# Low-rank attention of a two-block network: value products of two key tiles in the two column halves of the array, softmax denominators from GpSimd's sums

## The reference

```python
def mla_block(qn, qr, kn, kr, v):
    s = (jnp.einsum('bqhd,bkhd->bhqk', qn, kn) + jnp.einsum('bqhr,bkr->bhqk', qr, kr)).astype(jnp.float32) * MLA_SCALE
    p = jax.nn.softmax(s, axis=-1).astype(v.dtype)
    return jnp.einsum('bhqk,bkhd->bqhd', p, v)

def mla_latent(qn, qr, kn, kr, v):
    out = lax.map(lambda a: mla_block(a[0], a[1], kn, kr, v), (to_blocks(qn), to_blocks(qr)))
    return from_blocks(out)
```

## Time and profile before

| | us |
|---|---|
| median of the runs shown (3 runs) | 4291.66 |
| lowest, highest | 4281.98, 4299.93 |
| the profiled execution | 4297.97 |
| its span in the trace | 4296.1 |
| stage of the change, layer 0 (506.9 to 775.0) | 268.1 |
| stage of the change, layer 1 (1913.5 to 2154.3) | 240.8 |

### The profile page before, as it was taken

One profiled execution on the slowest core, in us unless ns is written; L12 is line 12 of the kernel. 1 busy time (PEld: TensorE's weight loads), 2 busy tenths in 40 slices (PEclk: granted clock), 3 DMA queues, 4 the chain that ended last, 5 costly groups with the idle time before them and its releaser, 6 DMA issues. The chain is left out here.

```text
span 4296.1 us, 51403 instructions
## 1 busy us (share of the span) xinstructions
PE 3948.0 (92%) x20691; PEld 3101.0 (72%) x20691; DVE 2079.7 (48%) x3243; ACT 1274.4 (30%) x2169; POOL 511.4 (12%) x601
## 2 busy tenths in 40 slices
PE   7989899988999899989996998899778999999997
PEld 5889565666777679866665998687555688887875
DVE  3466566333222256556535332683664465553444
ACT  3225433231111042553313333312453211112241
POOL 1010211102222110021012111100102100000011
PEclk9999899999999999889997999899788999999998
DMA  6100000448877431000025996112001211112111
GB/s 254 35 20 1 17 1 1 176 173 342 284 276 276 147 140 38 1 17 1 1 89 231 340 342 225 71 49 89 3 1 69 74 49 46 48 50 81 49 57 59
DMA packets 73876, 453.29 MB, mean 106 GB/s; under 512 B 8000, under 2 KB 12624, under 8 KB 57680
## 3 DMA queue, kind: packets, MB, share of 16 engines
q1 hardware_dynamic: 56960, 389.73, 24.1%
q0 software_dynamic: 13088, 47.19, 4.0%
q10 hardware_dynamic: 3632, 13.63, 0.8%
HBM read 394.95 MB, written 55.57 MB: 105 GB/s over the span
## 5 line engine op out<-in xcount | busy, mean ns | idle before, releaser
L2349 PEld LDWEIGHTS psum<-words,words 128*128 128x128 f32 x4096 | 510.9, 191 | 10.3 <-issue 9.1
L2349 PE MATMUL psum<-words,words 128*128 128x160 f32 (+1 forms) x4096 | 512.2, 287 | 1.6 <-DVE words L398 0.9
L682 PE MATMUL psum<-words,words 128*128 128x512 f32 x1104 | 440.7, 399 | 14.2 <-DVE words L722 9.8
L684 PE MATMUL psum<-words,words 128*128 128x512 f32 x1104 | 437.4, 396 | 0.0
L683 PE MATMUL psum<-words,words 128*128 128x512 f32 x1104 | 436.9, 396 | 0.0
L682 PEld LDWEIGHTS psum<-words,words 128*128 128x128 f32 x1104 | 208.7, 189 | 66.9 <-DVE words L722 11.4
L1658 PE MATMUL psum<-words,words 128*128 128x428 f32 (+1 forms) x720 | 253.2, 352 | 4.0 <-DVE words L1751 4.0
L1366 PE MATMUL psum<-words 128*128 128x512 f32 (+1 forms) x504 | 254.0, 586 | 0.0
L1659 PE MATMUL psum<-words,words 128*128 128x428 f32 (+1 forms) x720 | 248.7, 345 | 0.0
L1660 PE MATMUL psum<-words,words 128*128 128x428 f32 (+1 forms) x720 | 248.2, 345 | 0.0
L701 ACT ACTIVATE words<-words 128x1024 fp32r<-128x1024 f32 x69 | 73.1, 1060 | 581.0 <-DMA words<-in_w_up 382.2
(11 more groups left out here) (441 smaller groups left out, 7844.5 us busy)
## 6 DMA issues: line engine op xcount, KB each, us to landing
words<-in_w_gate SPq DMA_DIRECT2D x32, 2048.0 KB, 8.1
words<-in_w_up SPq DMA_DIRECT2D x32, 2048.0 KB, 12.5
words<-in_w_down SPq DMA_DIRECT2D x32, 2048.0 KB, 12.9
words<-in_ada_w SPq DMA_DIRECT2D x24, 2048.0 KB, 14.8
words<-in_w_in SPq DMA_DIRECT2D x55, 512.0 KB, 3.5
words<-in_w_up SPq DMA_DIRECT2D x44, 512.0 KB, 3.5
words<-in_w_down SPq DMA_DIRECT2D x44, 256.0 KB, 2.6
words<-in_x SPq DMA_DIRECT2D x2, 5120.0 KB, 22.4
```

What stands on the lines that cost most here:

```text
L682: pe.matmul(out, hi[:, j, w], S.parts[0](kt, t0, nt), start=(kt == 0), stop=False)
L684: mm = pe.matmul(out, lo[:, j, w], S.parts[0](kt, t0, nt), start=False, stop=(kt == KD - 1))
L2349: mm = pe.matmul(k.bank[m % 2][:, u * W:(u + 1) * W], ring[:, side[j], w0:w0 + P], xgT[:, j, kt, 0:W], start=(kt == 0), stop=(kt == KD - 1))
```

## The change

All of it lies in `latent_attention`.

- **Value products.** V's columns are now the 64 values alone (the ones stay in memory unused here). Products of even key tiles write rows 0 to 63 of O_BANK, those of odd ones rows 64 to 127. They are issued in batches of up to 4 key tiles: tiles 0 to 3 in the unit's fifth step, 4 to 7 in its ninth, 8 and 9 in the next unit's first. The two halves hold two sums that still have to be added.
- **Denominators.** POOL adds the probabilities of a unit's tiles into `acc` (9 chained additions of 128x512 per unit), and PE makes one fp32 product of `acc` with ones (`denominators`), into a bank of its own, D_BANK. For it S_BANK falls from three banks to two. The ring of probabilities grows from 4 to 7.
- **Outputs.** ACT copies rows 0 to 63 of O_BANK to SBUF (`lower_half`); DVE takes the reciprocals of D_BANK (128 rows where it was 64), adds the upper half to the copy, and multiplies the sum by the reciprocals: three instructions for each half of the queries where there were two. A table of steps (`when`, `out_at`) sets where DVE does it.
- **Remainders** of the next head's operands (`rests`) move from POOL to DVE, at steps 7 and 9 of a head. The row of ones of `k_hi` is now written by POOL, no longer by ACT.

```diff
-    H, R, LAG, ROW = 6, 4, 2, MLA_ROW
+    H, R, LAG, ROW, BATCH = 6, 7, 1, MLA_ROW, 4
...
-    S_BANK, C_BANK, O_BANK, M_BANK = (0, 1, 2), (3, 4), (5, 6), 7
+    S_BANK, D_BANK, C_BANK, O_BANK, M_BANK = (0, 1), 2, (3, 4), (5, 6), 7
+    batches = [(u, t, min(t + BATCH, units[u][3])) for u in range(N) for t in range(0, units[u][3], BATCH)]
+    batch_of = {begin[u] + t: i for i, (u, t0, t1) in enumerate(batches) for t in range(t0, t1)}
+    issued = {begin[u] + t1 - 1 + LAG: i for i, (u, t0, t1) in enumerate(batches)}
...
+    for u in range(N):
+        when.append(max(begin[u + 1] + 2, when[-1] + 4 if when else 0))
+    whole = {when[u]: u for u in range(N)}
+    lower = {when[u] + 1: u for u in range(N)}
+    out_at = {when[u] + 2 + half: (u, half) for u in range(N) for half in range(2)}
...
-                if p >= 3:
-                    pe.wait_ge(a_max, p - 2)
+                if p >= 2:
+                    pe.wait_ge(a_max, p - 1)
...
-            def values(x):
+            def values(i):
...
-                pe.matmul(k.bank[O_BANK[u % 2]][:, 0:n], V[:, 6 * t + h, :], pt[:, x % R, 0:n],
-                          start=(t == 0), stop=(t == keys - 1)).then_inc(d_done, 1)
+                pe.wait_ge(p_set, begin[u] + end)
+                for t in range(first, end):
+                    mm = pe.matmul(k.bank[O_BANK[u % 2]][64 * (t % 2):64 * (t % 2) + 64, 0:n], V[:, 6 * t + h, 0:64],
+                                   pt[:, (begin[u] + t) % R, 0:n], start=(t < 2), stop=(t >= keys - 2), skip_group_check=True)
+                mm.then_inc(d_done, 1)
+
+            def denominators(u):
+                n = units[u][2]
+                pe.wait_ge(summed, sums_in[u + 1])
+                if u:
+                    pe.wait_ge(rec_set, 2 * u)
+                pe.matmul(k.bank[D_BANK][:, 0:n], k.ones[:, :], acc[:, u % 2, 0:n], start=True, stop=True).then_inc(den_full, 1)
...
+            for x in range(END):
+                if x < len(steps):
+                    u, t = steps[x]
+                    exact(x)
+                if x in whole:
+                    denominators(whole[x])
+                if x < len(steps):
+                    for p in share(u, t):
+                        rough(p)
+                    if t == ripe(u) and u + 1 < N:
+                        shift_rows(u + 1)
+                if x in issued:
+                    values(issued[x])
...
+            def lower_half(u):
+                n = units[u][2]
+                act.wait_ge(den_full, u + 1)
+                act.wait_ge(d_done, batch_of[begin[u + 1] - 1] + 1)
+                act.activation(acc[64:P, u % 2, 0:n], k.bank[O_BANK[u % 2]][0:64, 0:n], ACT.Copy).then_inc(low_set, 1)
...
                 if x >= R:
-                    act.wait_ge(d_done, x - R + 1)
+                    act.wait_ge(d_done, batch_of[x - R] + 1)
+                    act.wait_ge(summed, added(x - R))
...
+            for b in range(2):
+                pool.memset(k_hi[ROW:ROW + 1, b, :].bitcast(F32), 1.0).then_inc(one_set, 1)
+            for x, (u, t) in enumerate(steps):
+                if t == 0:
+                    continue
+                n = units[u][2]
+                pool.wait_ge(p_set, x + 1)
+                if t == 1 and u >= 2:
+                    pool.wait_ge(o_out, 2 * (u - 1))
+                if t > 1:
+                    pool.wait_ge(summed, sums_in[u] + t - 1)
+                total = pt[:, (x - 1) % R, 0:n] if t == 1 else acc[:, u % 2, 0:n]
+                pool.tensor_tensor(acc[:, u % 2, 0:n], total, pt[:, x % R, 0:n], ALU.add).then_inc(summed, 1)
...
-                dve.wait_ge(d_done, begin[u + 1])
-                dve.reciprocal(rec[0:64, c], bank[64:P, c]).then_inc(rec_set, 1)
+                dve.wait_ge(den_full, u + 1)
+                dve.reciprocal(rec[:, c], k.bank[D_BANK][:, c]).then_inc(rec_set, 1)
+                dve.wait_ge(low_set, u + 1)
+                dve.tensor_tensor(to, k.bank[O_BANK[u % 2]][64:P, c], acc[64:P, u % 2, c], ALU.add).then_inc(joined, 1)
+                dve.wait_ge(joined, 2 * u + half + 1)
                 dve.wait_ge(rec_set, 2 * u + half + 1)
-                dve.tensor_tensor(MIX[64 * (h % 2):64 * (h % 2) + 64, h // 2, t0 + c.start:t0 + c.stop], bank[0:64, c], rec[0:64, c],
-                                  ALU.mult).then_inc(o_out, 1)
+                dve.tensor_tensor(to, to, rec[mine, c], ALU.mult).then_inc(o_out, 1)
...
+            rest_at = {begin[first_of[h - 1]] + 7 + 2 * part: (h, part) for h in range(1, H) for part in range(2)}
...
+            for x in range(END):
+                if x in out_at:
+                    outputs(*out_at[x])
+                if x in rest_at:
+                    rests(*rest_at[x])
+                if x < len(steps):
+                    for p in share(*steps[x]):
+                        maximum(p)
```

## The result

| | before | after |
|---|---|---|
| median of the runs, us | 4292.4 (4 runs, 4282.0 to 4299.9) | 4450.0 (4 runs, 4443.8 to 4452.9) |
| ratio | 1 | 1.0364 [1.0345, 1.0383] |
| span of the profiled execution, us | 4296.1 | 4449.2 |

The change makes the kernel slower by 157.5 us. The forecast was 4372, with a range up to 4425: the sign was right, the loss twice as large as expected. In the kernel after, the lines are: `rough` L1348, `shift_rows` L1356, `exact` L1368 to L1370, `values` L1379, `denominators` L1388, exponentials L1441, POOL's additions L1461, maxima L1470, the diagonal L1475, L1477, L1481, outputs L1490, L1492, L1495, remainders L1504, L1506.

A forecast was written before the change was run, and what follows sets the result against it. PE, busy 92%, was the bound; its 2.5 us saving a unit was outweighed by waits for DVE: layer 1 +19.5 to +32.6, layer 0 +46 to +67, total +65 to +99, taken as +80: 4372 us, range 4320 to 4425.

The forecast's parts named there:

- Value products, denominators: PE's work per unit: value batches fall from 8.6 to 5.24 us, denominators add 0.86; 15.84 in all, a gain of 2.5.
- The DVE chain: Layer 1: PE waits for DVE's maxima, outputs and diagonal; units without remainders take 19.9 us, with them 21.3, unblocked.
- POOL beside DVE: POOL's additions hold up DVE's two-SBUF-operand instructions, 0.4 to 0.6 us each; blocked, layer 1 units take 20.9, with remainders 22.9.
- unit G0: Layer 0, a head's first large unit, behind unit C: waits at pieces and shift row; 25.7 us, 28.7 if blocked by POOL.
- a clock of 0.5 inside the units: Sign that would show the prediction wrong: PE's granted clock at 0.5 within the units.
- Layer 0: Heads of three units, C, G0, G1: 50.35 us against 41.45, +8.9 a head, blocked +12.9; layer +46 to +67.
- POOL itself isn't late: Nine additions a unit, 12.6 us, end some 1.5 us into the next unit; denominators are asked for at 3.19.
- unit C: Layer 0, a head's small first unit: behind it PE waits for ACT, 4.65 us before and after; its batch gains nothing.
- unit G1: Layer 0, a head's second large unit: a plain unit with two more short pieces, 20.0 us against 18.4.
- The clock falls as well: Rival: half-speed stretch of 6 us in each layer-0 head, 3 us of PE work each; 4400 to 4412, chance 0.12.
- The halves run side by side: Value batches in two halves at once; the rival denied it: batches 3.76 and 2.04 us, 4412, chance 0.05.
- nothing was absorbed: Answers the rival that about half of the waits are absorbed: time within 20 us of 4292, chance 0.08.

The follow-up runs named there:

- the one with three sums: Kernel after plus three piece banks, value batches first, one reciprocal a unit; remainders on DVE at a head's second unit, three sum buffers, earlier outputs: 4274.5 us.
- the best version: The one with three sums, with a unit's first pieces ahead of its first exact product and outputs before a context unit one step apart: 4264.2 us, 0.9923.
- the fillers: Kernel after with unread bf16 products on PE ahead of its waits, in a bank freed by denominators sharing the shift row's: 4426.7 us, 1.0307.
- a version without the other waits: Kernel after plus three piece banks, value batches first, one reciprocal a unit, and remainders on DVE at the start of a head's second unit: 4309.7 us.
- the narrow sums: Kernel after with all but the first of POOL's nine additions a unit cut to 16 columns, leaving out most of each sum: 4445.4 us, 1.0359.

## Why the prediction was too low

- **Value products, denominators:** right. A batch of four tiles was to take 2.03 us and one of two 1.18; the next instruction follows 1.86 us behind (2070.64 to 2072.50 in the kernel after) and 1.01 (2041.43 to 2042.44 in the one with three sums); with 0.08 more ahead of a batch and 0.10 behind its first successor, that is 2.04 and 1.19. In the best version a unit takes 16.8 us where 15.84 was counted.
- **The DVE chain:** right, in place and nearly in size: in a plain unit waits of 0.30, 2.58 and 1.47 us for 0.36, 2.64 and 1.07. With remainders the last is 1.29 for 2.5, since PE comes later to the shift row.
- **POOL beside DVE:** right in kind and size. Without the hold a plain unit waits 1.7 us less, where the forecast had 1.0 between its two bounds; the time didn't follow, because of the clock. What was missed is the instruction with one input: L1477 wasn't on the list of those held up, and it stands right ahead of the diagonal. L1481, the diagonal itself, was on it and took its 0.69 us every time.
- **The failed step is the clock.** The prediction kept PE at full clock in every unit, and had the half clock only as a rival, only in unit G0 of layer 0 and with 3 us a head; it did name a clock of 0.5 inside the units as a sign of being wrong. In the run the clock fell in nearly every unit. It had set the clock of 0.98 in a stretch with PE busy 69% against such a fall; that row gives a busy share and doesn't say how long a single wait was. The size: in layer 1 the fillers give back 19.5 us of the 58.7, and 1.60 and 2.4 us beyond a wait of 1.81 and of 3.78 were measured by themselves. With 2.1 a unit on top (24.0 on average in the kernel after, 21.9 with the fillers), the forecast's 19.9 to 20.9 and 21.3 to 22.9 become 22.0 to 23.0 and 23.4 to 25.0; measured 23.1 and 24.6.
- **Layer 0** was forecast at +46 to +67 and came to +89.7; heads took 57.4 to 60.6 us after the first, where 50.4 to 54.4 was forecast. Beside the clock (0.80), "POOL itself isn't late" failed here. It holds for two large units in a row, but behind unit C the first addition needs a buffer that the outputs free 12.5 us later. The share of the two can't be told exactly: the fillers gained nothing there, while three buffers and earlier outputs gained 27.6 us in a version without the other waits. For the clock alone there is an estimate from unit G1: it takes 23.0 us and more with one wait of 3.0, where the same work took 18.19 with one of 1.60 at a clock of 1.00, so at least 3.4 us a head are the clock.
- **The rivals:** "The clock falls as well" was the nearest by mechanism (4400 to 4412) and too small in place and price. The halves run side by side, and nothing was absorbed.

Of the gain of 2.5 us a unit that the change was after, the best version shows 1.8 in layer 1 (16.8 for 18.6). It appears once DVE has less to do in front of the pieces and PE has something else to issue where DVE is late.

## What to carry to other kernels

When an edit moves work from the engine that is the bound to the one that feeds it, follow one period of the schedule and list the single waits, not the sums. Then price a wait of TensorE at more than its own length, since the matmuls behind it may run at half clock. What was seen here beyond the waits, a unit: nothing for one of 0.5 to 0.8 us; between nothing and 4.8 us for the same wait of 1.60; 1.6 for 1.81, in all nine units; 2.4 for 3.78; 2.0 for 1.31 and 0.77 close together; some 4, by estimate (23.4 less the waits of 2.7 and the 16.6 of a unit without waits), for 2.32 and 0.37 with the narrow sums. It isn't a fixed price, and a shorter wait isn't always a cheaper one: carry it as a range. And where the feeding engine is later still, the half clock costs nothing until that engine has caught up. The cheapest cures here were orders, not less work: independent products in front of the instruction that waits, and long side work where the feeding engine is idle anyway.

## What the runs showed of the hardware

- TensorE's granted clock fell to its lower level (1.2 of 2.4 GHz) behind waits of 1.81 us, one a unit, with work on both sides, for 3.5 us, and not at once: the products at 2023.54 to 2025.7 still ran near full clock (start-to-start 0.23 to 0.24), the batch at 2025.70 took 1.98 instead of 1.08. Waits of up to 0.8 us, one a unit, left the clock at 1.00. Behind the same wait of 1.60 us, in one execution, it stayed at 1.00 in two of five units and fell in three.
- DVE instructions with two SBUF operands can be held for the rest of a POOL instruction whatever their own length: 2.55 us for one of 0.42. A `tensor_scalar` on 128x4 from SBUF is held too (0.17 to 1.2, and 0.17 each time with the narrow sums), while in the kernel after a reduction of 128x12 from SBUF (L1475, 0.17) and the reciprocal of 128x256 from PSUM (1.75) never were.
- Moving a head's two subtractions from DVE (3.8 us in layer 1) to POOL (5.2) made the kernel no faster, and layer 1 slower by 9.5 us, though DVE was the engine that PE waited for.
